# Block one of a two-block transformer layer: values of two head pairs in one insertion, the third pair's probabilities turned by VectorE, one scaling a step sooner

## The reference, cut to what matters

```python
def hybrid_layer(x, ...):
    xn = rms_norm(x, norm1_g)
    proj = xn @ w_in     # q, keys and values, gates, conv_b, conv_c, conv_x, gate_a, gate_b
    ...
    # selected and windowed attention; with 256 rows both are plain causal attention over all rows,
    # with slopes * distance taken from the scores (8 heads of 64, 2 key-value heads)
    o_nsa = g[:, :, 0] * o_cmp + g[:, :, 1] * o_slc + g[:, :, 2] * o_win
    u = conv_c * conv_x
    z = conv_b * conv(u, conv_w)                      # 3 taps, per channel
    mixed = (sigmoid(gate_a) * (o_nsa @ w_branch_a)
             + sigmoid(gate_b) * (z @ w_branch_b))
    x = x + mixed @ w_out
    h = rms_norm(x, norm2_g)
    return x + square(relu(h @ w_up)) @ w_down
```

## Time and profile before

| | |
|---|---|
| median of 3 runs | 902.04 us (901.62 to 902.25) |
| the profiled execution | 901.26 us, span 899.2 us, 2.06 us lie outside the span |
| PE busy | 892.7 us (99%) |
| DVE busy | 706.0 us (79%) |
| ACT busy | 555.3 us (62%) |
| POOL busy | 43.2 us (5%) |
| DVE busy, 80 to 120 us / 120 to 160 us | 34.81 / 37.84 of 40 us |
| mean granted clock of TensorE | 0.999 |

### The profile page before, as it was taken

How to read it: one execution, slowest core, us unless ns; L and a number is a source line. 1 busy time by engine, 2 the same in 40 slices (tenths; PEclk the granted TensorE clock), 3 DMA queues, 4 the chain that set the end, 5 groups by cost and what they waited for, 6 DMA issues and landing times.

```text
span 899.2 us, 13582 instructions
## 1 busy us (share of the span) xinstructions
PE 892.7 (99%) x4926; PEld 767.0 (85%) x4926; DVE 706.0 (79%) x1381; ACT 555.3 (62%) x954; POOL 43.2 (5%) x54
## 2 busy tenths in 40 slices
PE   9999999999999999999999999999999999999997
PEld 7988877888888888888889998888889988888886
DVE  6888899789866666677998999999976786666665
ACT  7767878755644444456655657776745755754454
POOL 0410000000000000000010100100000000000000
PEclk9999999999999999999999999999999999999999
DMA  9977677676465555556798888487565377555551
GB/s 343 320 214 199 177 203 219 198 293 202 154 229 187 192 191 196 190 191 209 219 236 268 231 206 270 106 230 240 169 211 164 114 212 237 187 187 187 188 188 47
DMA packets 97218, 184.53 MB, mean 205 GB/s; under 512 B 8128, under 2 KB 18176, under 8 KB 96896
## 3 DMA queue, kind: packets, MB, share of 16 engines
q1 hardware_dynamic: 92128, 166.35, 56.1%
q0 software_dynamic: 4656, 16.78, 10.0%
q10 hardware_dynamic: 368, 0.52, 0.2%
HBM read 164.69 MB, written 1.05 MB: 184 GB/s over the span
## 4 chain that ended last, share of the span: by engine, by line
PE 99%; ACT 1%; issue 0%; DVE 0%; DVEq 0%; ACTq 0%
PE pb L523 97%; PE pb L527 1%; PE pb L738 1%; ACT SM L1400 0%; ACT wlo L1174 0%; ACT SM L1174 0%; ACT whi L1174 0%; ACT PTC L1174 0%; DVE XS L2617 0%; DVE XS L2625 0%; DVEq L59 0%; DVE DG L2359 0%; ACT MSQ L1757 0%; DVE ST L2603 0%; ACT CC L1174 0%
## 5 line engine op out<-in xcount | busy, mean ns | idle before, releaser
L1174 ACT ACTIVATE whi<-raw 128x1024 fp32r<-128x1024 f32 (+2 forms) x304 | 309.1, 1039 | 125.5 <-PE pb L523 112.5
L1787 DVE TENSOR_TENSOR wlo<-raw,whi 128x1024 fp32r<-128x1024 f32 (+1 forms) x267 | 315.7, 1211 | 78.7 <-ACT whi L1174 78.2
L523 PE MATMUL pb<-XT,whi 128*128 128x512 f32 (+1 forms) x1232 | 283.8, 358 | 0.0
L523 PE MATMUL pb<-whi,ZO 128*128 128x512 f32 (+1 forms) x776 | 238.9, 388 | 0.0
L523 PEld LDWEIGHTS pb<-XT,whi 128*128 128x128 f32 x1232 | 200.8, 189 | 23.8 <-issue 1.4
L523 PEld LDWEIGHTS pb<-whi,ZO 128*128 128x128 f32 x776 | 145.2, 188 | 29.7 <-issue 0.4
L523 PE MATMUL pb<-XT,wlo 128*128 128x256 f32 (+1 forms) x1032 | 166.4, 282 | 0.0
L523 PEld LDWEIGHTS pb<-XT,wlo 128*128 128x128 f32 (+1 forms) x1032 | 153.2, 190 | 14.0
L523 PE MATMUL pb<-whi,XT 128*128 128x512 f32 (+1 forms) x544 | 161.8, 389 | 0.0
L523 PE MATMUL pb<-wlo,ZO 128*128 128x512 f32 (+1 forms) x388 | 148.3, 387 | 0.0
L523 PEld LDWEIGHTS pb<-whi,XT 128*128 128x128 f32 x544 | 101.0, 188 | 20.7 <-issue 0.7
(11 more groups left out here) (258 smaller groups left out, 657.9 us busy)
## 6 DMA issues: line engine op xcount, KB each, us to landing
raw<-in_w_in SPq DMA_DIRECT2D x105, 512.0 KB, 4.8
raw<-in_w_ff SPq DMA_DIRECT2D x64, 512.0 KB, 5.3
raw<-in_w_up SPq DMA_DIRECT2D x32, 512.0 KB, 4.5
raw<-in_w_down SPq DMA_DIRECT2D x32, 512.0 KB, 4.8
wlo<-raw POOLq DMA_DIRECT2D x31, 512.0 KB, 5.8
raw<-in_w_branch_b SPq DMA_DIRECT2D x8, 512.0 KB, 5.3
raw<-in_w_out SPq DMA_DIRECT2D x8, 512.0 KB, 4.1
raw<-in_wx_kv SPq DMA_DIRECT2D x8, 512.0 KB, 5.4
```

What stands on the lines that cost most here:

```text
L523: return e.matmul(o, l, r, start=start, stop=stop, skip_group_check=True)
L1174: return e.activation(o, i, ACT.Copy, scale=scale)
L1787: e.tensor_tensor(wlo[u % NW][:, 0:c], raw_tile(u)[:, 0:c], whi[u % NW][:, 0:c].bitcast(F32), ALU.subtract).then_inc(lo, 1)
```

## The change

It has three parts, all in block one.

1. `values_of` is now 22: (0, 1), 29: (2, 3), 35: (4, 5), 42: (6, 7). The values of the even pairs wait for those of the odd ones: three insertions (steps 19, 26, 32) lose a set of values and three (22, 29, 35) gain one. A third buffer for the turned pairs (`PT`, at W0 + 7216) holds what has to wait, and the waits on `pv_done` count accordingly.
2. Pair 2 (j = 4, 5) leaves `by_pe`. Two `turn_item` (three turns each, TensorE, in steps 19 and 22) and two `copy_p` (ScalarE, steps 21 and 23) go; VectorE turns 16 blocks, eight in step 21 and eight in step 22, each time before all else that VectorE has in that step. The order on VectorE in step 21 is then: 8 blocks, `pair_factors` of pair 3, `taps1`, `make_z`, `make_lo` of unit 37; in step 22: 8 blocks, `taps1`, `make_z`, `make_lo` of unit 38; in step 23 as before.
3. `scale_p(0, 0)`, the scaling of j = 0, moves on ScalarE from step 14 to step 13, ahead of the two roundings of a `by_dma` unit. TensorE turns j = 0 in the insertion of step 13, behind the scores of pair 1.

```diff
-        PTP = [work(W0 + a, f"PT{i}", 768) for i, a in enumerate((12016, 14840))]
+        PTP = [work(W0 + a, f"PT{i}", 768) for i, a in enumerate((12016, 14840, 7216))]
...
+        def pt1(j):
+            return PTP[j // 2 % 3][:, 384 * (j % 2):384 * (j % 2) + 384]
...
-        values_of = {a: (i,) for i, a in enumerate(pair_at[3:] + (35,))}
-        values_of[42] = (6, 7)
-        last_value = {a: n[-1] // 2 for a, n in values_of.items() if n[-1] % 2}
-        blocks_of = {pair_at[n] + 5 + i: (n, i) for n in (3, 4, 5, 6, 7) for i in range(3)}
-        by_pe = [j for j in range(16) if j // 2 not in (3, 4, 5, 6, 7)]
+        values_of = {22: (0, 1), 29: (2, 3), 35: (4, 5), 42: (6, 7)}
+        last_value = {a: n[0] // 2 for a, n in values_of.items()}
+        blocks_of = {pair_at[n] + 5 + i: (n, a, b) for n in (3, 4, 5, 6, 7)
+                     for i, (a, b) in enumerate(((0, 6), (6, 11), (11, 16)))}
+        blocks_of[pair_at[2] + 5], blocks_of[pair_at[2] + 6] = (2, 0, 8), (2, 8, 16)
+        by_pe = [j for j in range(16) if j // 2 not in (2, 3, 4, 5, 6, 7)]
...
-                            mm(PB[7][64 * p:64 * p + 64, 0:256], QKV[:, 0, v0:v0 + 64], PT[(2 * n + p) % 4][:, 0:256],
+                            mm(PB[7][64 * p:64 * p + 64, 0:256], QKV[:, 0, v0:v0 + 64], pt1(2 * n + p)[:, 0:256],
...
-                    if s - 4 in pair_of:
+                    if s == 13:
+                        scale_p(0, 0)
+                    if s - 4 in pair_of and s > 14:
                         scale_p(2 * pair_of[s - 4], 0)
...
-                if base + j >= 4:
+                if base:
                     e.wait_ge(pv_done, base + j - 3)
-                copy(PT[j % 4][:, :], PB[5 if base else 6][:, 0:384]).then_inc(pt_out, 1)
+                elif j >= 6:
+                    e.wait_ge(pv_done, j - 5)
+                copy(PT[j % 4] if base else pt1(j), PB[5 if base else 6][:, 0:384]).then_inc(pt_out, 1)
...
-                        n, part = blocks_of[s]
-                        if part == 0:
+                        n, first_block, end_block = blocks_of[s]
+                        if first_block == 0:
                             e.wait_ge(sc_p, 2 * n + 2)
-                            e.wait_ge(pv_done, 2 * n - 2)
-                        for m in range((0, 6, 11)[part], (6, 11, 16)[part]):
+                            if n > 2:
+                                e.wait_ge(pv_done, 2 * n - 4)
+                        for m in range(first_block, end_block):
                             a, b = m // 4 * 32, m % 4 * 32
-                            i = e.transpose(PT2[n % 2][b:b + 32, :, a:a + 32], SM2[n % 2][a:a + 32, :, b:b + 32])
-                        if part == 2:
+                            i = e.transpose(PT3[n % 3][b:b + 32, :, a:a + 32], SM2[n % 2][a:a + 32, :, b:b + 32])
+                        if end_block == 16:
                             i.then_inc(p_blocks, 1)
```

More of the change, by code:

```diff
@@ L106, in build @@
         SMP = [work(W0 + 10480 + 768 * i, f"SM{i}", 768) for i in range(2)]
-        PTP = [work(W0 + a, f"PT{i}", 768) for i, a in enumerate((12016, 14840))]
+        PTP = [work(W0 + a, f"PT{i}", 768) for i, a in enumerate((12016, 14840, 7216))]
         SM, PT = ([v[i // 2][:, 384 * (i % 2):384 * (i % 2) + 384] for i in range(4)] for v in (SMP, PTP))
-        SM2, PT2 = ([v[i][:, :].rearrange("p (c n) -> p c n", c=6) for i in range(2)] for v in (SMP, PTP))
+        SM2, PT3 = ([v[:, :].rearrange("p (c n) -> p c n", c=6) for v in b] for b in (SMP, PTP))
+        def pt1(j):
+            return PTP[j // 2 % 3][:, 384 * (j % 2):384 * (j % 2) + 384]
         CC = [work(W0 + a, f"CC{i}", 1024)[:, :].rearrange("p (f n) -> p f n", f=4) for i, a in enumerate((12784, 16240))]
@@ L907, in attention1 @@
                             mm(PB[7][64 * p:64 * p + 64, 128:256], QKV[:, 1, v0:v0 + 64],
-                               PT[(2 * n + p) % 4][:, 256:384], False, False).then_inc(pv_done, 1)
+                               pt1(2 * n + p)[:, 256:384], False, False).then_inc(pv_done, 1)
                         if b == 1:
```

## The result

The changed kernel takes 908.16 us (median of 6 runs, 907.3 to 909.03); the kernel before, measured beside it, 901.96 us (6 runs, 901.62 to 902.5). The ratio is 1.0068, 95% interval 1.0055 to 1.0081: 0.7% slower. The prediction was 907.9 us.

A forecast was written before the change was run, and what follows sets the result against it. TensorE, busy 892.7 us of 899.2, bounds the kernel, so its new waits count in full. Unit 36 +3.86, steps 26 to 35 -0.30 and the clock +2.3 give +5.9 on 902.04: 907.9 us, range 904.9 to 909.9.

The forecast's parts named there:

- Scaling sooner, -0.43 us: Step 13: ScalarE's scaling is done before TensorE asks, gaining 0.43 us (bounds 0.37 and 0.44).
- TensorE earns 1.22 us before unit 36: Of TensorE's own -1.52 us, 1.22 are earned before unit 36, then lost in the wait.
- 16 blocks, 6.05 us, less 1.04 of idle time: VectorE, steps 21 and 22: new work less idle time makes what follows 5.01 us later, 4.58 after the 0.43 gain.
- The wait of 5.1 us at unit 36: TensorE stands still 5.1 us until `add_right` frees bank 2; unit 36 begins 3.86 us later.
- The clock, 2.3 us: The clock falls in the wait at unit 36, costing 2.3 us; wait with fall of the clock 0.60.
- the second bank: At unit 36, f = 1 comes 0.79 us later, costing 0 to 0.3 us more; taken as 0.
- a clock that holds: Rival: the wait at unit 36 comes, the clock stays full, +3.6 to +3.9, 905.8 us; chance 0.22.
- The bound of 2.6: Upper bound of the clock's loss, 2.6 us, from the start of the kernel: 5.3 us at half speed.
- Steps 26 to 35, -0.30 us: Steps 26 and 32 each lose 0.80 us of values, 29 and 35 each gain 0.65: -0.30 us together.
- Sum: Whole kernel: +3.86 (unit 36) - 0.30 (steps 26 to 35) + 2.3 (clock) = +5.9 us.
- the slack would shrink by 0.7 us: Behind the wait, VectorE some 4.6 us late and TensorE 3.9, so the low parts' slack shrinks by 0.7 us.
- the smallest slack at the low parts of the weights: Unit 44: the low part has 4.8 us of slack, of which 4.1 remain, so no wait there.

The follow-up runs named there:

- kept_busy: The changed kernel with ten products whose result nobody reads, on TensorE ahead of unit 36; 906.33 us, ratio to before 1.0047.
- 8 + 8: The kernel before with 8 more VectorE blocks in step 21 and 8 in step 22, into a buffer nobody reads; 909.36 us, ratio 1.0085.
- 6 + 6: The kernel before with 6 more VectorE blocks in step 21 and 6 in step 22, into a buffer nobody reads; 907.5 us, ratio 1.0057.
- outs_first: The changed kernel with VectorE taking out `b1_b1` ahead of pair 2's second eight blocks and all of step 23; 905.64 us, ratio 1.0049.
- pair2_by_tensor: The changed kernel with pair 2 given back to TensorE; merged values, third buffer and early scaling stay; 901.72 us, ratio 0.9997.

## Why the prediction was right

Step by step, with the sizes that the prediction gave:

- *Scaling sooner, -0.43 us.* In the changed kernel the turn of j = 0 starts 0.86 us after the scores (81.83 to 82.69), before 1.29 us: -0.43. Alone, the part is worth 0.33 us from step 10 to the end.
- *TensorE earns 1.22 us before unit 36.* The product behind step 22 begins at 114.07 in both traces, 1.20 us sooner once the start is taken off.
- *16 blocks, 6.05 us, less 1.04 of idle time.* Measured 3.05 and 3.09 us from the blocks to what follows, 6.14 in all; `add_right` starts at 121.72, which is 4.70 us late with the start taken off, where 4.58 was predicted.
- *The wait of 5.1 us at unit 36.* The profile says 5.15 us, counted from the modelled end of the last product. Counted as the prediction did, from where the first product of unit 36 could have started (about 116.97), it is 5.3. Unit 36 begins 4.12 us later than before ((122.28 - 71.97) - (116.96 - 70.77)), predicted 3.86. Of the 0.26 us between them 0.12 are the blocks, and 0.14 the time from the end of `add_right` (122.14) to the first product (122.28), which I had counted as nothing.
- *The clock, 2.3 us.* Unit 36 takes 5.25 us against 2.73: 2.52 us. It was the least certain term, a choice between 0 and 2.6, and `kept_busy` shows that it is a real one: 2.0 us by the traces, about the 2.52 less what the second bank costs at a full clock (3.10 - 2.73 = 0.37). All six runs of the changed kernel lie above the 905.8 us of a clock that holds. That it came out so near was partly luck: the same term was 2.8 and 3.0 us in the traces with 8 + 8 and 6 + 6 blocks. The bound of 2.6 took all products up to 5.26 as run at exactly half speed. With the 0.224 us that one such record takes in `kept_busy` (4.48 for 20) I estimate that the start lost 4.07 - 2.24 + 0.60 = 2.4 us; the trace of the changed kernel has a start that lost only 1.8 by the same sum (1.19 to 4.98, then 4.98 to 7.04).
- *Steps 26 to 35, -0.30 us.* From unit 37 to the values of step 42: 127.53 to 183.91 is 56.38 us, before 119.69 to 176.29 is 56.60: -0.22.
- *Sum.* 4.12 + 2.52 - 0.22 = 6.42 us, the traces have 6.40, the medians 6.2; predicted 5.9.

Two statements of the prediction were not quite right. The first is on VectorE's lateness further down. I had TensorE 3.9 us late and VectorE 4.6, so that the slack would shrink by 0.7 us, and left my own clock term out of it: with the half clock TensorE was 6.6 us late, and the slack grew. And I had looked for the smallest slack at the low parts of the weights (4.8 us), where `negated` in front of step 29 has 2.3; `outs_first` shows the wait that comes there when TensorE is not held up first. The second is the price of TensorE's own work. Without the blocks its terms give a gain of 0.43 + 0.45 us, but they leave out the copy that the values of pair 0 had covered (0.51 us, `pair2_by_tensor`). Inside the change itself this did not matter, since the second turn of step 19 had gone as well.

The rule of the Trainium skill in "VectorE: DVE Perf Modes", section "Rules for kernel authors", that a 128x128 transpose is TensorE's work, agrees with the outcome: the changed kernel with pair 2 turned by TensorE gives 0.9997, with VectorE's blocks 1.0068. The runs show it where VectorE has little idle time; none of them tried it where VectorE is idle.

## What to carry to other kernels

When work moves from the busiest engine to one that is 79% busy, do not price it by that share: walk along the second engine's program from the place of the new work to the next thing that the first one waits for, and count idle time and slack on the way. Here the way was 1.8 us wide (1.04 + 0.72) and the work 6.05 us long. Price a long wait of TensorE at its length and the half clock on top: here waits of 2.8 to 5.15 us at unit 36 cost 2.5 to 3.0 us in this way in their traces, though one execution with 2.8 us seems to have gone without. What TensorE alone saved ahead of the wait was worth nothing here; what let VectorE start sooner too was kept. And after removing one wait look for the next place at which the same lateness arrives.

## What the runs showed of the hardware that I had not expected

- How soon the clock falls was not the same each time: about 2.2 us after the last product with 6 + 6 blocks (117.65 to 119.8), 3.4 us with 8 + 8 (118.43 to 121.8), 3.6 us in the changed kernel, 2.7 us at the end of the kernel before. In `outs_first` it fell 1.5 us after a wait of 2.84 us was over. It held in waits of 0.5, 0.8 and 1.3 us.
- The way back to the full clock took 5.3 us of products in the changed kernel, 5.8 with 8 + 8 blocks (122.81 to 128.6), 6.2 with 6 + 6 (120.48 to 126.6) and 5.0 in `outs_first` (137.44 to 142.4, of which 3.4 at half clock). That the start of the program is slow for as long is read from the length of its products alone (0.41 us for a record that takes 0.224 in `kept_busy`): the granted clock in the profile reads 1.00 there.
- Ten products that nobody needs (4.48 us of TensorE's time) in a wait that was there anyway kept the clock at 1.00, and the kernel with them was 1.8 us faster than the changed one without.
- Ahead of step 10, where all of these kernels have the same instructions, the profiled executions differ by up to 1.3 us (step 10 begins between 70.74 and 72.07). That is more than the gain of any part of this change, so differences under a microsecond were read from step 10 on.
